# Two stacked transformer blocks on one core: squares of the MLP output taken with its last quarter, the result stored in pieces, tiles moved by 160 bytes, and x loaded and summed before the memory

## What is computed

```python
def rmsnorm(x, g):                     # over the features of a token
    return x * rsqrt(mean(x * x) + 1e-6) * g

def first_block(x, mem, ...):          # 2 layers
    h = rmsnorm(x, norm_mix_pre[l])    # statistics of x: the very first step
    ...                                # pools, convolution, dilated attention, gates
    mem_n = rmsnorm(mem, norm_memkv[l])            # 256 memory tokens
    x = x + rmsnorm(memory_cross_attention(h, mem_n, ...), ...)
    ...                                # gated MLP
def second_block(x, c, ctx, ...):      # 2 layers; 256 context tokens ride along in layer 0
    ...                                # mixers
    f_x = squared_relu_mlp(modulate(rms_norm(x, g[2]), ...), w_mlp_in[l], w_mlp_out[l])
    x = x + g2_x * rms_norm(f_x, g[3])
```

## Time and profile before

| | |
|---|---|
| median of 3 runs | 3855.02 us (3854.51 to 3859.83) |
| the profiled execution | 3854.92 us, span of its instructions 3853.1 us |
| PE busy | 3642.8 us, 95% of the span |
| DVE, ACT, POOL busy | 2007.3, 1508.5, 241.6 us |
| transfers | 333 MB, mean 86 GB/s |
| share of the chain that ended last | PE 82%, DVE 7%, ACT 6% |

### The profile page before, as it was taken

How to read it: one execution, slowest core, us unless ns; L and a number is a source line. 1 busy time by engine, 2 the same in 40 slices (tenths; PEclk the granted TensorE clock), 3 DMA queues, 4 the chain that set the end, 5 groups by cost and what they waited for, 6 DMA issues and landing times.

```text
span 3853.1 us, 52811 instructions
## 1 busy us (share of the span) xinstructions
PE 3642.8 (95%) x19430; PEld 2974.7 (77%) x19430; DVE 2007.3 (52%) x3383; ACT 1508.5 (39%) x2303; POOL 241.6 (6%) x384
## 2 busy tenths in 40 slices
PE   7999989999999998899999888899999898889997
PEld 5788877887787887688778776788888787668885
DVE  4634466777763445677773565433233344644443
ACT  4344354332324535533244366422122335742322
POOL 0000000001000000000000151000000002610000
PEclk9999999999999999999999999999999999999999
DMA  3222222446322223144541101111111121212222
GB/s 124 98 72 88 96 85 82 146 140 199 114 98 77 83 99 104 55 142 147 192 133 61 44 12 31 44 60 60 66 61 65 38 71 49 30 44 92 93 93 71
DMA packets 112574, 333.14 MB, mean 86 GB/s; under 512 B 32680, under 2 KB 33576, under 8 KB 111784
## 3 DMA queue, kind: packets, MB, share of 16 engines
q1 hardware_dynamic: 73472, 264.18, 20.5%
q0 software_dynamic: 14400, 52.44, 4.2%
q10 hardware_dynamic: 24552, 14.51, 1.7%
HBM read 328.99 MB, written 6.00 MB: 87 GB/s over the span
## 4 chain that ended last, share of the span: by engine, by line
PE 82%; DVE 7%; ACT 6%; issue 2%; DVEq 1%; POOL 0%; ACTq 0%; POOLq 0%; DMA 0%; SPq 0%
PE PS L595 14%; PE PS L597 13%; PE PS L596 13%; PE PS L970 11%; PE PS L969 10%; PE PS L972 10%; PE PS L670 2%; PE PS L1097 1%; PE PS L756 1%; ACT PB L1653 1%; ACT FULL_P L1653 1%; ACT L1351 1%; PE PS L768 1%; DVE Y L2345 1%; DVE WL L1887 1%
## 5 line engine op out<-in xcount | busy, mean ns | idle before, releaser
L1887 DVE TENSOR_TENSOR WL<-RAW,WH 128x1024 fp32r<-128x1024 f32 x494 | 604.5, 1224 | 572.1 <-ACT WH L1315 565.5
L1315 ACT ACTIVATE WH<-RAW 128x1024 fp32r<-128x1024 f32 x494 | 521.4, 1056 | 658.2 <-PE PS L972 369.2
L595 PE MATMUL PS<-HHI,WH 128*128 128x512 f32 x1632 | 645.8, 396 | 25.2 <-DVE HLO L1924 17.5
L597 PE MATMUL PS<-HHI,WL 128*128 128x512 f32 x1632 | 641.9, 393 | 0.0
L596 PE MATMUL PS<-HLO,WH 128*128 128x512 f32 x1632 | 641.0, 393 | 0.0
L969 PE MATMUL PS<-H2HI,WH 128*128 128x512 f32 (+1 forms) x1336 | 471.2, 353 | 0.0
L970 PE MATMUL PS<-H2LO,WH 128*128 128x512 f32 (+1 forms) x1336 | 450.4, 355 | 0.0
L595 PEld LDWEIGHTS PS<-HHI,WH 128*128 128x128 f32 x1632 | 307.0, 188 | 109.9 <-issue 23.4
L972 PE MATMUL PS<-H2HI,WL 128*128 128x512 f32 (+1 forms) x1336 | 387.8, 350 | 0.0
L596 PEld LDWEIGHTS PS<-HLO,WH 128*128 128x128 f32 x1632 | 307.4, 188 | 66.1 <-issue 0.5
L597 PEld LDWEIGHTS PS<-HHI,WL 128*128 128x128 f32 x1632 | 307.3, 188 | 64.6
(11 more groups left out here) (350 smaller groups left out, 5769.0 us busy)
## 6 DMA issues: line engine op xcount, KB each, us to landing
RAW<-in_stream SPq DMA_DIRECT2D x494, 512.0 KB, 3.3
MODW<-in_modw POOLq DMA_DIRECT2D x96, 512.0 KB, 3.6
bias_rows<-in_rpb ACTq DMA_DIRECT2D x8, 476.2 KB, 6.6
MEM<-in_mem ACTq DMA_DIRECT2D x3, 1024.0 KB, 4.7
X<-in_x SPq DMA_DIRECT2D x1, 2048.0 KB, 9.1
CROW<-in_crow POOLq DMA_DIRECT2D x4, 512.0 KB, 4.6
out<-X SPq DMA_DIRECT2D x1, 2048.0 KB, 7.1
BIAS<-bias_rows ACTq DMA_DIRECT2D x8, 224.0 KB, 4.8
```

The costliest lines, as they stand in the source:

```text
L595: nc.tensor.matmul(out, WH[:, slot, b * P:(b + 1) * P], hi, start=start, stop=False)
L597: return nc.tensor.matmul(out, WL[:, slot, b * P:(b + 1) * P], hi, start=False, stop=stop)
L1315: A(WH[:, d, :], RAW[:, s, :], ACT.Copy).then_inc(high_split, 1)
L1887: TT(WL[:, d, :], RAW[:, s, :], WH[:, d, :].bitcast(F32), ALU.subtract).then_inc(split_ready, 1)
```

## The change

Four things. (1) In block two the last quarter of the MLP is taken out of the loops of ACT and DVE: as each of its eight chunks of Y2 is added, ACT squares it and DVE adds the square to ACC, so that PE needs one `statistics` in place of `sum_squares`, in both layers. (2) The result is stored in five pieces, each as soon as its chunks are ready. (3) One line rounds the place of H2LO up by 160 bytes, and with it all tiles behind. (4) X is loaded in four pieces ahead of PAR and the rest, and squared piece by piece; MEM is loaded last of the first transfers, from SP; its squares (MEM_SQ) stand behind the norm of layer 0 on ACT, its sums behind the first two units on PE, its root behind the first two outputs on ACT.

```diff
+        MEM_SQ = place("MEM_SQ", [P, KB, TC], at=ZB + KB * T)
...
+        at2[0] = Z + -(-(at2[0] - Z) // 64) * 64
         H2LO = place2("H2LO", [P, KB, TA], F32R)
...
@@ block.sync
-            sp.dma_start(X[:], x).then_inc(x_in, 16)
-            sp.dma_start(PAR[:], params1).then_inc(x_in, 16)
+            for j in range(4):
+                sp.dma_start(X[:, 2 * j:2 * j + 2, :], x[:, 2 * j:2 * j + 2, :]).then_inc(x_part[j], 16)
+            sp.dma_start(PAR[:], params1).then_inc(par_in, 16)
...
+            sp.dma_start(MEM[:], mem).then_inc(mem_in, 16)
...
-            sp.wait_ge(x_ready, DEPTH * 3 * KB + DEPTH * 2 * KB)
-            sp.dma_start(out.rearrange("(k p) t -> p k t", p=P), X[:]).then_inc(stored, 16)
+            pieces = ((0, 2), (2, 4), (4, 6), (6, 7), (7, 8))
+            for k0, k1 in pieces:
+                sp.wait_ge(x_ready, DEPTH * 3 * KB + DEPTH * 2 * KB - KB + k1)
+                sp.dma_start(result[:, k0:k1, :], X[:, k0:k1, :]).then_inc(stored, 16)
@@ block.tensor
+            def memory_sums():
+                for k in range(KB):
+                    m.add("sq")
+                    pe.wait_ge(sq_ready, m.at("sq"))
+                    nc.tensor.matmul(FLAT[:, 6 * T:6 * T + TC], ONES[:], MEM_SQ[:, k, :], start=k == 0, stop=k == KB - 1).then_inc(sq_summed, 1)
-            pe.wait_ge(x_in, 16 * 4)
-            sum_squares(TC, 0)
+            pe.wait_ge(ones_in, 32)
             sum_squares(T, 0)
...
                 chunk_pair(HHI, HLO)
+                if l == 0:
+                    memory_sums()
...
-                sum_squares(TA if full else T)
+                statistics(TA if full else T)
@@ block.scalar
+            def memory_squares():
+                act.wait_ge(mem_in, 16)
+                for k in range(KB):
+                    A(MEM_SQ[:, k, :], MEM[:, k, :], ACT.Square, scale=D ** -0.5).then_inc(sq_ready, 1)
+                m.add("sum", KB)
+            def memory_root():
+                act.wait_ge(sq_summed, m.at("sum"))
+                inverse_root(MR[:], FLAT[:, 6 * T:6 * T + TC]).then_inc(mr_ready, 1)
+            act.preload_act_table(ACT.Ln)
+            act.wait_ge(ones_in, 32)
             squares_summed(of_x0, T)
...
                 norm_high()
+                if l == 0:
+                    memory_squares()
                 for c in range(2):
                     take(U[:, c, :].unsqueeze(1))
                 if l == 0:
+                    memory_root()
                     act.wait_ge(ang_ready, 1)
...
+                hidden_high()
+                for k in range(KB):
+                    p = unit_wait()
+                    split_high()
+                    m.add(f"use{p}")
+                    dst = square_slot(k)
+                    act.wait_ge(taken[p], m.at(f"use{p}", 1))
+                    A(dst[:, 0:n2], Y2[:, k, 0:n2], ACT.Square, scale=D ** -0.5).then_inc(y_squared, 1)
+                m.add("sqt", KB - 1)
                 act.preload_act_table(ACT.Ln)
-                squares_summed(of_y3, n2)
-                root(n2, summed=True)
+                root(n2)
@@ block.vector
+                hidden_squared()
+                for k in range(KB):
+                    output_added(slice(k, k + 1), k % 2)
+                    if k < KB - 1:
+                        split_low()
+                    if k:
+                        add_squares(k - 1, n2, y_square_arrived)
+                add_squares(KB - 1, n2, y_square_arrived)
+                split_low()
+                dve.drain()
                 root_inverse(n2)
                 residual2(l, 5, full)
```

More of the change, by code:

```diff
@@ L414, in build @@
         high_split, split_ready, units_done = sem("high_split"), sem("split_ready"), sem("units_done")
-        x_in = sem("x_in")
+        ones_in, par_in, x_part = sem("ones_in"), sem("par_in"), [sem(f"x_part{j}") for j in range(4)]
         taken = [sem("taken0"), sem("taken1")]
@@ L1400, in attention @@
                     A(PTS[:, n % 2, 0:n_keys], FLAT[:, 4 * T:4 * T + n_keys], ACT.Copy).then_inc(pts_ready, 1)
[L1402 to L1409, removed]
             def of_x0(k, dst, n):
+                if k % 2 == 0:
+                    act.wait_ge(x_part[k // 2], 16)
                 A(dst[:, 0:n], X[:, k, :], ACT.Square, scale=D ** -0.5).then_inc(sq_ready, 1)
-            root(TC, summed=True)
+            def memory_squares():
[8 more added lines that the diff above has]
+            act.wait_ge(ones_in, 32)
             squares_summed(of_x0, T)
@@ L1417, in _ @@
                 split_high()
-            act.wait_ge(mr_ready, 1)
             root(T, summed=True)
@@ L1841, in _, with hidden_high @@
                 norm_high2(l, 3, full)
-                with m.loop(act, QUARTERS, units=2 * KB, use0=KB, use1=KB, val=KB, w=2 * KB, **{name: 2 * KB // RAW_SLOTS for name in RAW_LAPS}):
+                def hidden_high():
                     with m.loop(act, KB // 4, units=4, use0=2, use1=2, val=4, **QUAD) as i:
@@ L1851, in _ @@
                             A(GHI[:, bass.ds(4 * i + c, 1), 0:n2], TMP[:, p:p + 1, 0:n2], ACT.Copy).then_inc(hi_ready, 1)
+                with m.loop(act, QUARTERS - 1, units=2 * KB, use0=KB, use1=KB, val=KB, w=2 * KB, **{name: 2 * KB // RAW_SLOTS for name in RAW_LAPS}):
+                    hidden_high()
                     with m.loop(act, KB // 4, units=4, **QUAD):
@@ L1983, in _ @@
             nc.vector.memset(DEN[:], 0.0).then_inc(taken[1], 1)
-            dve.wait_ge(x_in, 16 * 4)
+            dve.wait_ge(ones_in, 32)
+            dve.wait_ge(par_in, 16)
             m.add("sq", 2 * KB)
-            m.add("root")
-            dve.wait_ge(root_ready, m.at("root"))
-            nc.vector.tensor_copy(MR[:], RS[:, 0:TC]).then_inc(mr_ready, 1)
             for _ in range(SPLIT_AHEAD):
@@ L2151, in _ @@
                         dve.wait_ge(mem_in, m.at("mem", 16))
+                        dve.wait_ge(mr_ready, 1)
                         for k in range(KB):
@@ L2535, in _, with hidden_squared @@
                 dve.wait_ge(y_zero, l + 1)
-                with m.loop(dve, QUARTERS, units=2 * KB, use0=KB, use1=KB, relu=KB, hi=KB, w=2 * KB, **{name: 2 * KB // RAW_SLOTS for name in RAW_LAPS}):
+                def hidden_squared():
                     with m.loop(dve, KB // 4, units=4, use0=2, use1=2, relu=4, hi=4, **QUAD) as i:
@@ L2552, in _, with output_added, y_square_arrived @@
                             dve.drain()
+                def output_added(k, p):
+                    m.add("units")
+                    m.add(f"use{p}")
+                    dve.wait_ge(units_done, m.at("units"))
+                    y = Y2[:, k, 0:n2]
+                    TT(y, y, FLAT[:, 3 * p * T:3 * p * T + n2].unsqueeze(1), ALU.add).then_inc(taken[p], 1)
+                def y_square_arrived(k):
+                    dve.wait_ge(y_squared, l * KB + k + 1)
+                with m.loop(dve, QUARTERS - 1, units=2 * KB, use0=KB, use1=KB, relu=KB, hi=KB, w=2 * KB, **{name: 2 * KB // RAW_SLOTS for name in RAW_LAPS}):
+                    hidden_squared()
                     with m.loop(dve, KB // 4, units=4, use0=2, use1=2, **QUAD) as i:
                         for c in range(4):
[L2555 to L2560, removed]
+                            output_added(bass.ds(4 * i + c, 1), c % 2)
                             split_low()
                     dve.drain()
-                dve.drain().then_inc(y_ready, 1)
+                hidden_squared()
+                for k in range(KB):
[7 more added lines that the diff above has]
+                dve.drain()
                 root_inverse(n2)
```

15 lines of the change are left out of this document (6 added, 9 removed).

## The result

The change takes **3810.7 us** (median of 4 runs, 3807.1 to 3813.1), where the kernel before took 3855.1 (4 runs, 3854.5 to 3859.8): ratio 0.9881, 95% interval 0.9864 to 0.9898. That is 44.4 us less between the medians; the profiled execution of the change took 3807.1 us (span 3805.3), 47.8 less than the profiled one before. The forecast was 3811.

A forecast was written before the change was run, and what follows sets the result against it. PE, holding 82% of the chain, was taken to bound the kernel. Start -11.2, MLP ends -7.7 and -9.7, store -4.1 and homes -11 sum to -43.7 us: from 3855.0 to 3811, range 3797 to 3829.

The forecast's parts named there:

- The start: Loading x first: root of x 15.4 us earlier, 4.2 lost to the memory's later work, net -11.2 us.
- The one more sum at the lower clock: At the start, PE takes one more sum of x at 1.2 GHz than before, 0.9 us.
- The memory's root: Behind layer 0's norm, ACT's root of the memory delays the sines; PE waits: 4.2 us lost, bounds 3 and 5.5.
- The step that failed: At PE's fourth unit: the whole chain moves by 4.2 us and PE waits for it, 4.2 us lost.
- The MLP ends: Block two's MLP ends, squares taken unit by unit: -7.7 us in layer 1, -9.7 in layer 0; bounds together 15 and 18.5.
- the row of the mixer: Profile row behind a mixer, squares taken unit by unit: last product to root takes 5.8 us.
- The store: End of program, result stored in pieces: last piece takes 2.7 us plus 0.3; -4.1 us, bounds 1.5 and 4.6.
- The homes: Block two's moved tiles let PE step faster on H2 and GHI: -11 us, bounds +2 and -18.
- The rival at 0.37: Moved tiles in block two do nothing, something other than place sets PE's step: 3822 us, chance 0.37.
- The pieces of x: Rival: transfers queue at 3.3 us each, start loses 1.5 us and the store 5.5 more: 3818 us, chance 0.05.
- The slower step everywhere: Rival: the new start sets block one's 6912 main matmuls to the slower step, 37 us more: 3863 us, chance 0.04.

The follow-up runs named there:

- start_only: The kernel before with only the new loads, squares and root of x and the memory behind: 3843.8 us, ratio 0.9969.
- pieces_only: The kernel before with only the result stored in five pieces: 3850.7 us, ratio 0.9989.
- homes_only: The kernel before with only the line that moves H2LO and all tiles behind it by 160 bytes: 3841.8 us, ratio 0.9969.
- no_homes: The change without the line that moves H2LO and the tiles behind it: 3821.3 us, ratio 0.9915.
- square_first: The change with the last square of Y2 ahead of the last weight split on ACT, both layers: 3809.3 us, ratio 0.9877.
- all_plus32: The change with every large tile of both blocks 32 bytes further: 3853.9 us, ratio 0.9997.
- homes_plus32: The change with H2LO and the tiles behind it 32 bytes further, 224 past a multiple of 256: 3820.9 us, ratio 0.9912.
- late_root: The change with the memory's root behind the two sines on ACT: 3802.8 us, ratio 0.9860.
- both_late_first: The change with the memory's root behind the sines and the last square ahead of the last split: 3800.7 us, ratio 0.9854.

## Why the prediction was right, and where it was not

**The start: 11.2 predicted, 8.6 found.** The root of x was put at 19.4 and came at 20.45 (19.42 in start_only). Most of the difference is the first piece: put at 5.0 to 5.4, it let the first square begin at 6.09. The row of 3.3 us that I took for 512 KB was of single transfers in a running stream; here the first of four pieces issued close together took 4.3. COL did not stand in the way, it landed in 1.9 us. The one more sum at the lower clock was about right: from the first sum to the end of the last square 9.1 us, predicted 8.8. The memory's root was priced at 4.2 and cost 4.1 in COS. **The step that failed** is the sentence that the whole chain moves by 4.2 and PE waits for it: I did not ask what the longer pause does to PE. It was 2.5 us before and 4.3 after, and PE came back at half speed, 1.6 us more. 10.2 + 1.0 would have been 11.2; 1.0 and 1.6 are the whole miss. The fourth unit itself came 29.6 us behind the root, exactly as forecast.

**The MLP ends: 17.4 predicted, 17.3 found.** Roots 7.8 and 6.3 us behind the last product predicted, 8.0 and 6.5 found. Costing the chain operation by operation, with the row of the mixer as a check, was the best method of the whole prediction.

**The store: 4.1 predicted, 4.9 found.** The last piece took 2.1 us to land, not 2.7 + 0.3: the slope from 2 MB to 512 KB gave too much for 256 KB. As the prediction drew it from the Trainium skill, "SBUF — State Buffer", section "The DMA setup-cost knee", the fixed part of a transfer speaks against pieces. The measured 2.8 us for 512 KB and 2.1 for 256 KB do hold a large part that doesn't shrink with the size, 1.4 us if the difference of 0.7 is what 256 KB cost, but in pieces_only it passes beside the work of DVE for all pieces but the last. To take the largest single transfer, which that section of the Trainium skill asks of DMA-bound transfers, would have cost 4.9 us here, where the data become ready piece by piece.

**The homes: 11 predicted, 14.2 found.** The reading of 173, 175 and 177 matmuls in equal windows was right, and homes_only and no_homes show it from both sides. Layer 0 was taken with 5 and had 7.2; layer 1 with 6 and had 7.1. The rival at 0.37, by which the homes do nothing, rested on FHI, which runs at 173 in layer 0 at its good place. That observation was true and is a second effect (below). The Trainium skill's 16-byte lines ("SBUF — State Buffer", section "Specifications (TRN2)"), by which 32 past is as good as 192, do not describe what PE does here: by that rule homes_only would be at 3855, and it is at 3842.

**The other rivals.** The pieces of x did not take 3.3 us behind one another; they landed 1.3 us apart, as the prediction's own sum has it. The slower step everywhere did not come with the change, but one stretch had it at its good place with the new start, in start_only and square_first (below), and all_plus32 shows that it exists and that moving every tile by 32 bytes brings it: 43 us by the medians, where the rival had 52.

**The sum.** The terms found are 8.6 + 17.3 + 4.9 + 14.2 = 45.0, against 43.7 predicted and 44.4 measured between the medians. So 3811 is close also because a start that was 2.6 us too good stood against homes and a store that were 4 us too small. The profiled execution lies 3.6 below the median of its kernel; the other three were not traced, so what made them slower isn't known, but it is no more than the scatter described at the end.

## What to carry to other kernels

A matmul stream that never pauses can still be some 2% from its best: count the matmuls that begin in equal windows for each tile, and where one tile's count is lower at the same clock, try it at the residue of the good ones; here that took one line. Which residues are good was measured for this kernel's fp32 streams alone. When work is moved behind a critical point, look at which queue it now stands ahead of: a root that is read 330 us later must not stand before the sines that DVE waits for, and a pause of PE costs more than its length when PE restarts at the lower clock. And take an edit worth 1 or 2 us from its chain in the trace, not from medians of runs that scatter by 5 us to each side.

## What the runs showed of the hardware that was not expected

**A place 32 bytes away costs 2% of PE.** Steps of 233.3 to 234.3 ns in place of 228.9, for tiles 32, 64 and 224 bytes past a multiple of 256 in place of 192; the change and homes_plus32 differ in nothing but 32 bytes. The good step is a pattern of 226, 229 and 232 ns.

**A good place is not enough.** FHI, at 192 in 13 of the 14 traced kernels, ran at 232.3 or 233.3 ns in 6 of its 26 streams (two per execution), among kernels that don't differ there; late_root has it in layer 0, both_late_first in both layers. It isn't FHI alone: in start_only and square_first HHI ran at 233.2 ns from the fourth unit to the end of its first stretch, some 565 matmuls. Here are windows on FHI of late_root, layer 0 and layer 1, then on that first stretch of HHI in start_only and in the change:

```profile
900.00:940.00 40.00, 40.00 (x173) 32.40 (x172) 31.56 (x51) 11.40 (x14) 4.22 (x8) 1.00 0.64 207
1896.00:1936.00 40.00, 40.00 (x177) 32.81 (x176) 30.36 (x50) 10.42 (x12) 4.22 (x8) 1.00 0.66 210
...
110.00:150.00 40.00, 40.00 (x173) 32.37 (x173) 27.89 (x43) 10.82 (x14) 0.00 (x0) 1.00 0.28 92
...
110.00:150.00 40.00, 40.00 (x177) 32.81 (x176) 28.56 (x45) 10.82 (x14) 0.00 (x0) 1.00 0.29 94
```

Each such stream costs 1.8 to 2.4 us. All eight began with a restart of PE at the lower clock; but 15 FHI streams that began so ran at the good step, so what starts it is open. What can be seen is that the step changes where PE restarts and then holds: in start_only HHI goes from 229.3 to 233.3 ns at the pause before the fourth unit, and in homes_only and pieces_only it goes from 233.3 to 229 behind the pauses at 52 to 62 us, over the same tiles at the same place.

**A restart of PE falls to 1.2 GHz or not, behind the same pause.** At the MLP of block one, layer 1, PE waits 3.5 us in both kernels. Before, then the change:

```profile
1859.00:1862.00 3.00, 2.77 (x7) 2.19 (x8) 1.04 (x3) 0.00 (x0) 0.53 (x1) 0.50 0.99 366
```

```profile
1851.00:1854.00 3.00, 2.98 (x13) 2.49 (x14) 0.83 (x3) 0.00 (x0) 0.53 (x1) 1.00 0.93 342
```

That is 2.5 us, and it is not the change's doing. The 14 traces have 28 restarts behind such a pause of 3.5 us (one in each layer of block one): 5 went on at the full clock, 23 with 5 to 11 matmuls 427 ns apart. In all, some 50 to 80 of the main matmuls of an execution are 427 ns apart, which at 0.2 us each makes 10 to 16 us. This and the slow streams are together about as large as the scatter of one kernel's runs (3849.7 to 3860.1 for the kernel before in the first set); that they are its cause isn't shown.
